# A two-layer hybrid decoder trunk on one core: boundaries reordered, modulation pieces behind the tile, level differences on VectorE, stick-breaking sums in two rounded parts

## The reference, cut to what matters

```python
def modulated_sublayer(x, fn, g_pre, g_post, m, res_w):
    shift, scale, gate = m[:, 0][:, None], m[:, 1][:, None], m[:, 2][:, None]
    h = rms_norm(x, g_pre) * (1.0 + scale) + shift
    return x + res_w * gate * rms_norm(fn(h), g_post)

for l in range(DEPTH):
    mod = (silu(c) @ w_ada[l] + b_ada[l]).reshape(bsz, 3, 3, D_MODEL)   # the modulation
    x = modulated_sublayer(x, ffn1,   ..., mod[:, 0], 0.5)   # (silu(h @ wa) * (h @ wb)) @ w_out
    x = modulated_sublayer(x, mixing, ..., mod[:, 1], 1.0)
    x = modulated_sublayer(x, ffn2,   ..., mod[:, 2], 0.5)
```

```python
log_1m = where(causal, log_sigmoid(-z), 0)            # minus the softplus of z
suffix = cumsum(log_1m, reverse=True) - log_1m
a = where(causal, exp(log_sigmoid(z) + suffix), 0);   o = a @ v
```

## Time and profile before

| | |
|---|---|
| median of three runs | 3118.58 us |
| the profiled execution's own time, and its span | 3121.1 us, 3119.3 us |
| mean granted TensorE clock | 0.975 of 2.4 GHz |
| PE busy | 2929.9 us (94%) |
| PE weight loads busy | 2558.1 us (82%) |
| DVE busy | 1541.3 us (49%) |
| ACT busy | 1005.0 us (32%) |
| POOL busy | 193.1 us (6%) |
| DMA | 324.53 MB, 104 GB/s on average |

### The profile page before, as it was taken

One profiled execution on the slowest core, in us unless ns is written; L12 is line 12 of the kernel. 1 busy time (PEld: TensorE's weight loads), 2 busy tenths in 40 slices (PEclk: granted clock), 3 DMA queues, 4 the chain that ended last, 5 costly groups with the idle time before them and its releaser, 6 DMA issues.

```text
span 3119.3 us, 40607 instructions
## 1 busy us (share of the span) xinstructions
PE 2929.9 (94%) x16999; PEld 2558.1 (82%) x16999; DVE 1541.3 (49%) x2236; ACT 1005.0 (32%) x1455; POOL 193.1 (6%) x188
## 2 busy tenths in 40 slices
PE   6999898989999988999989989899899999899998
PEld 5888897777788788889988879877777887888897
DVE  5555236777344446542255552477753554453323
ACT  3322124444422323222242221354443232332212
POOL 1000001221100020000000000021211002000000
PEclk7999999999999999999999999999999999999999
DMA  6555331222112233542226542222111232343321
GB/s 238 176 189 189 109 96 61 61 62 68 41 55 82 81 127 104 189 135 95 97 88 195 186 167 89 88 62 75 51 52 41 68 95 81 109 122 95 102 89 55
DMA packets 358854, 324.53 MB, mean 104 GB/s; under 512 B 12300, under 2 KB 305552, under 8 KB 357776
## 3 DMA queue, kind: packets, MB, share of 16 engines
q1 hardware_dynamic: 357136, 319.77, 32.4%
q10 hardware_dynamic: 1536, 2.16, 0.2%
HBM read 313.43 MB, written 6.29 MB: 102 GB/s over the span
## 4 chain that ended last, share of the span: by engine, by line
PE 85%; DVE 7%; ACT 3%; issue 2%; POOL 0%; ACTq 0%; DVEq 0%; POOLq 0%
PE PS L769 25%; PE PS L771 24%; PE PS L770 24%; PE PS L973 2%; PE PS L786 2%; DVE WL L1573 1%; PE PS L1048 1%; PE PS L1010 1%; PE PS L1070 1%; PE PS L1034 1%; PE PS L1025 1%; PE PS L1022 1%; PE PS L832 1%; ACT WH L1164 1%; PE PS L779 1%
## 5 line engine op out<-in xcount | busy, mean ns | idle before, releaser
L769 PE MATMUL PS<-HH,WH 128*128 128x512 f32 (+1 forms) x2512 | 974.3, 388 | 27.3 <-DVE WL L1562 10.3
L771 PE MATMUL PS<-HH,WL 128*128 128x512 f32 (+1 forms) x2512 | 948.7, 378 | 0.0
L770 PE MATMUL PS<-HL,WH 128*128 128x512 f32 (+1 forms) x2512 | 946.9, 377 | 0.0
L1562 DVE TENSOR_TENSOR WL<-RAW,WH 128x2048 fp32r<-128x2048 f32 x142 | 325.5, 2292 | 515.5 <-ACT WH L1164 515.5
L769 PEld LDWEIGHTS PS<-HH,WH 128*128 128x128 f32 x2512 | 475.7, 189 | 116.7 <-DVE WL L1573 13.7
L771 PEld LDWEIGHTS PS<-HH,WL 128*128 128x128 f32 x2512 | 475.0, 189 | 88.7
L770 PEld LDWEIGHTS PS<-HL,WH 128*128 128x128 f32 x2512 | 476.1, 190 | 82.0 <-issue 2.9
L1164 ACT ACTIVATE WH<-RAW 128x2048 fp32r<-128x2048 f32 x142 | 271.8, 1914 | 792.6 <-PE PS L771 792.6
L769 PE MATMUL PS<-GH,WH 128*128 128x256 f32 x1408 | 405.0, 288 | 18.2 <-DVE WL L1562 17.5
L771 PE MATMUL PS<-GH,WL 128*128 128x256 f32 x1408 | 403.7, 287 | 0.0
L770 PE MATMUL PS<-GL,WH 128*128 128x256 f32 x1408 | 403.3, 286 | 0.0
(11 more groups left out here) (225 smaller groups left out, 3470.3 us busy)
## 6 DMA issues: line engine op xcount, KB each, us to landing
RAW<-in_ffn_w_in SPq DMA_DIRECT2D x176, 512.0 KB, 5.2
RAW<-in_w_in SPq DMA_DIRECT2D x132, 512.0 KB, 4.7
AW<-in_w_ada SPq DMA_DIRECT2D x248, 256.0 KB, 4.8
RAW<-in_ffn_w_out SPq DMA_DIRECT2D x88, 512.0 KB, 4.2
AWB<-in_w_ada SPq DMA_DIRECT2D x5, 2048.0 KB, 16.0
RAW<-in_w_out SPq DMA_DIRECT2D x16, 512.0 KB, 4.0
x_kept<-X SPq DMA_DIRECT2D x2, 2048.0 KB, 7.4
X<-x_kept SPq DMA_DIRECT2D x2, 2048.0 KB, 10.1
```

What stands on the lines that cost most here:

```text
L769: pe.matmul(o, ah, bh, start=start, stop=skip, skip_group_check=skip)
L770: pe.matmul(o, ah, bl, start=False, stop=skip, skip_group_check=skip)
L771: return pe.matmul(o, al, bh, start=False, stop=stop or skip, skip_group_check=skip)
L1562: dve.tensor_tensor(wl[:, 0:n], RAW[g % 2][:, 0:n], wh[:, 0:n].bitcast(F32), ALU.subtract).then_inc(w_low, 1)
```

## The change

- **Buffers of the groups at a boundary.** `from_stage` gives a group's distance d to a stage's end. The group of d = -2 now goes into WXH[0], d = -1 and d = 0 into the other parity's WH, d = 1 into WXH[1]; the groups waited for are 2, 3, 3, 4, 3, 3 back for d = -2 to 3.
- **Order at a boundary.** ACT squares the updated x two steps earlier and takes the second root of y after the first two inputs are rounded; PE's sums of x for the second half stand at k = 3 to 5 instead of 4 to 7; a `rows_product` begins with banks 6 and 7, and waits by quarters. After the mixing the wait for all eight gate products (`br_mul`) is split as well.
- **Modulation.** In the first feed-forward part of a layer, the last chunk's sum on PE and its copy on DVE move behind the boundary, to step (3, 0) of the mixing.
- **Mixing.** `a_diff` is issued by DVE, one level ahead; `take` stands before `a_prepare`, whose step 3 is cut in two; transposes of turned values stand a step later; tiles 4 to 7 have banks of their own; the first weight group of `merge` gets its low part at step 3 of the last item.
- **Stick-breaking sums.** ACT rounds the masked softplus to BH (`b_round`), DVE takes the rest to BSL (`b_lows`), and `b_args` multiplies both with rounded copies of the matrices (CR).

The diff, cut to its core (lines that are only "..." are left out):

```diff
-    def beside(g):
-        return g % NG in (G_MIX, G_MIX + 1, G_FFN2, G_FFN2 + 1) or (g % NG < 2 and now[0] + g // NG > 0)
+    def from_stage(g):
+        g += NG * (now[0] > 0)
+        return min((g - e - n * NG for n in range(3) for e in ROW_ENDS if g - e - n * NG >= -2), default=99)
     def free(g):
-        if beside(g):
-            back = max((e for e in ROW_ENDS if e <= g), default=0) - 3
-        else:
-            back = g - (4 if beside(g - 2) else 2)
+        d = from_stage(g)
+        back = g - {-1: 3, 0: 3, 1: 4, 2: 3, 3: 3}.get(d, 2)
     def halves_of(g):
-        return (WXH[g % 2], WXL[g % 2]) if beside(g) else (WH[g % 2], WL[g % 2])
+        d = from_stage(g)
+        if d in (-2, 1):
+            return WXH[d > 0], WXL[d > 0]
+        slot = (g + (d in (-1, 0))) % 2
+        return WH[slot], WL[slot]
     def bank(tile):
-        return tile if tile < 4 else tile % 2
+        return tile if tile < 8 else tile % 2
...
                 def first_pair(p, g0, done):
-                            if not half and p and (u, i) == (1, 1) and k >= KT // 2:
-                                x_sum(p, 1, k - KT // 2)
+                            if not half and p and (u, i) == (1, 1) and 3 <= k <= 5:
+                                x_sum(p, 1, k - 3)
+                                if k == 5:
+                                    x_sum(p, 1, 3)
...
-                        for half in (1, 0) if i == 0 else (0, 1):
-                            for j in range(KT):
-                                if i == 0 and bank_free:
+                        for half, j0 in ((1, 4), (0, 0), (0, 4), (1, 0)) if i == 0 else ((0, 0), (0, 4), (1, 0), (1, 4)):
+                            for j in range(j0, j0 + 4):
+                                if i == 0 and j == j0:
                                     bank_free(half, j)
...
                 def b_args(h):
-                    pe.wait_ge(b_spm, at(b_spm, h + 1))
+                    pe.wait_ge(b_low, at(b_low, h + 1))
                     for i in range(TT):
-                        mm = pe.matmul(PS[:, bank, col:col + P], ident, const("negm"), ...)
-                        mm = pe.matmul(PS[:, bank, col:col + zw(i)], const("ntri"), BS[h % 2][:, ZCOL[i]:ZCOL[i] + zw(i)], ...)
-                        for j in range(i + 1, TT):
-                            mm = pe.matmul(PS[:, bank, col + P * (j - i):col + zw(i)], const("nones"),
-                                           BS[h % 2][:, ZCOL[j]:ZCOL[j] + zw(j)], ...)
+                        pe.matmul(PS[:, bank, col:col + P], CR[:, 0, :], CR[:, 3, :], ...)
+                        for j in range(i, TT):
+                            for part in (BH, BSL[h % 2]):
+                                mm = pe.matmul(PS[:, bank, col + P * (j - i):col + zw(i)], CR[:, 1 if j == i else 2, :],
+                                               part[:, ZCOL[j]:ZCOL[j] + zw(j)], ...)
...
+                def merged_free(half, j):
+                    pe.wait_ge(br_mul, at(br_mul, {(1, 4): KT - 2, (0, 0): KT - 1}.get((half, j), KT)))
                 def merged(i):
-                    if i == 0:
-                        pe.wait_ge(br_mul, at(br_mul, KT))
...
                     for m in range(2, NM):
                         for k in range(8):
+                            if (m, k) == (3, 0):
+                                pe.wait_ge(*taken(2))
+                                ada(0, ADA_CHUNKS[0] - 1)
...
# ScalarE
+                def b_round(h):
+                    act.wait_ge(b_spm, at(b_spm, h + 1))
+                    act.wait_ge(b_arg, at(b_arg, h))
+                    act.activation(BH[:, :], BS[h % 2][:, :], ACT.Copy).then_inc(b_high, 1)
...
# VectorE
+                def a_diff(h, k):
+                    n = A_LEVELS * h + k
+                    dve.wait_ge(p_log, at(p_log, 3 * h + 3))
+                    dve.wait_ge(v_decay, at(v_decay, max(n - 1, 0)))
+                    ...
+                    dve.tensor_tensor(level_view(AD[n % 2][:, :], k), b, b[:, :, w // 2 - 1:w // 2].broadcast_to(...), ALU.subtract)
                 def a_head(h, k):
+                    if k == 0:
+                        a_diff(h, 0)
+                    if k + 1 < A_LEVELS:
+                        a_diff(h, k + 1)
+                def b_lows(h):
+                    dve.wait_ge(b_high, at(b_high, h + 1))
+                    dve.tensor_tensor(BSL[h % 2][:, :], BS[h % 2][:, :], BH[:, :].bitcast(F32), ALU.subtract).then_inc(b_low, 1)
```

More of the change, by code:

```diff
@@ L158 @@
 _at = 0
-for _name, _n in (("ident", P), ("ones", P), ("ntri", P), ("nones", P), ("strict", P), ("negm", P),
+for _name, _n in (("ident", P), ("ones", P), ("ntri", P), ("nones", P), ("negm", P), ("strict", P),
                   ("reset", SEQ), ("del0", TT * 2 * P), ("del1", P), ("del2", P)):
@@ L319, in body @@
     BS = [sb(f"BS{i}", [P, 1280], F32, r1 + 34816 + 5120 * i) for i in range(2)]
+    BSL = [sb(f"BSL{i}", [P, 1280], F32R, r1 + 34816 + 5120 * i) for i in range(2)]
+    BH = sb("BH", [P, 1280], F32R, r1 + 12480)
+    CR = sb("CR", [P, 4, P], F32R, r1 + 57344)
     BA = [sb(f"BA{i}", [P, 1280], F32, r1 + 45056 + 5120 * i) for i in range(2)]
@@ L825, in ffn_in @@
                     first_pair(p, g0, lambda i: (a_done, w_used)[i])
-                    def ada(i):
-                        pe.wait_ge(ada_part, at(ada_part, i * KT + (ADA_BEFORE[f] + 2) * KT))
-                        pe.wait_ge(ada_out, at(ada_out, ADA_BEFORE[f] + i))
-                        for q in range(4):
-                            mm = pe.matmul(PS[:, 4, q:q + 1], AACC[i % 2][:, q * P:(q + 1) * P], ones[:, 0:1],
-                                           start=True, stop=True)
-                        mm.then_inc(ada_sum, 1)
                     n = chunks(l, f)
@@ L842, in ffn_in, with ada, rows_product @@
                             if u and i <= n:
[L843 to L847 removed]
+                                ada(f, i - 1)
+                def ada(f, i):
+                    pe.wait_ge(ada_part, at(ada_part, i * KT + (ADA_BEFORE[f] + 2) * KT))
+                    pe.wait_ge(ada_out, at(ada_out, max(ADA_BEFORE[f] + i - 1, 0)))
+                    for q in range(4):
+                        mm = pe.matmul(PS[:, ada_bank(f, i), q:q + 1], AACC[i % 2][:, q * P:(q + 1) * P], ones[:, 0:1],
+                                       start=True, stop=True)
+                    mm.then_inc(ada_sum, 1)
+                def rows_product(g0, n, rh, rl, ready, b, bank_free):
                     def column(i, j, half):
[L851 to L852 removed]
+                        wh, wl = (w[:, :].rearrange("p (k c) -> p k c", k=2) for w in halves_of(g0 + i))
                         cols = HALVES[half]
@@ L936, in project @@
                     tile = TILE0[m] + i
-                    if k0 == 0:
+                    if k0 == 0 and tile >= 8:
                         pe.wait_ge(tile_out[tile % 2], at(tile_out[tile % 2], tile // 2))
@@ L1241, in boundary @@
                         square_y(b, 1, q)
-                        if q in (1, 2) and not last:
-                            square_x(b + 1, 0, 2 * q - 2)
-                            square_x(b + 1, 0, 2 * q - 1)
-                    root_y(b, 1)
+                        if q < 2 and not last:
+                            square_x(b + 1, 0, 2 * q)
+                            square_x(b + 1, 0, 2 * q + 1)
                     if last:
+                        root_y(b, 1)
                         return
@@ L1587, in ffn_in @@
                                 ada_columns(f, i - 2)
+                            if (i, u) == (FI // 2 - 1, 1) and n == FI // 2:
+                                ada_columns(f, i - 1)
                             if i < n:
                                 ada_pieces(f, i, u)
-                    for i in range(min(n, FI // 2 - 2), n):
-                        ada_columns(f, i)
                 def ffn_tile(f, g0, i, u):
@@ L1878, in mixers @@
                         take(m, 0)
-                    if k == 2 and m and TILE0[m] - 1 in TURN_OF:
+                    if (m, k) in PREPARE_AT:
+                        a_prepare(*PREPARE_AT[(m, k)])
+                    if k == 3 and TILE0[m] - 1 in TURN_OF:
                         take_turned(TILE0[m] - 1)
```

85 lines of the change are left out of this document (46 added, 39 removed).

## The result

| | before | after |
|---|---|---|
| median of four runs | 3120.92 us | 2975.87 us |
| profiled execution, its span | 3121.1, 3119.3 us | 2976.25, 2974.5 us |
| PE busy | 2929.9 us | 2875.6 us |
| DVE, POOL busy | 1541.3, 193.1 us | 1555.2, 93.4 us |
| mean granted TensorE clock | 0.975 | 0.987 |

The ratio is 0.9534, 95% interval 0.9517 to 0.9550. The forecast was 2959, its range 2930 to 3010: the time lies in the range, inside the likeliest case's own 2940 to 2982, and on the number of the rival with dear matmuls (2976), whose mechanism isn't what happened. Between the two profiled spans lie 144.8 us where I had 160.

The account below looks back on a forecast made before the run. PE was taken to bound the kernel: its columns, its waits and its stretches at 1.2 GHz. The terms sum to 160 us off the profiled 3121.1, giving 2961, less 2.5 between profile and median 2959; range 2930 to 3010.

Parts of the forecast that it names:

- likeliest case: Whole kernel: forecast as summed, 2959 us, own range 2940 to 2982, chance 0.68.
- rival with dear matmuls: Stick-breaking sums: 128-column matmuls cost 0.23 us each, 17 us less gained, 2976 us; chance 0.12.
- a to e: Last two groups' buffers 40.2 us, boundary squares 12, boundary inputs 22, modulation's last chunk 21.9, merge and w_out 17.6.
- b: Squares of x at boundaries: PE's 2.4 us wait on XSQ goes at each of five; gain 12.0 us.
- c: Next sublayer's inputs: pair sums to second half's first matmul, 19.0 us instead of 23.4, five boundaries; gain 22 us.
- e: merge and w_out: waits on the low part and on the eighth gate product go; gains 11 and 6.6 us.
- one gap of about 2 us: Sign at the boundaries: one such PE gap in the first half of `first_pair`, none before the second.
- f: Stick-breaking sums: a head takes 3.1 us instead of 5.15, 12 heads; gain 24.4 us.
- hidden: Softplus, mask, rounding and low part before the sums need some 10.5 us, covered by PE's some 14 us of other work.
- g: A heads: 5 us from level copies, 17 from tiles and low parts, 3 from the clock; gain 25 us.
- The boundary's chain: Rival at the boundaries: ACT's and DVE's lists set the pace, (a) to (c) give 40, not 74; 2993 us; chance 0.15.
- DVE lost in the heads: Rival in A heads: the one level of lead is lost, 185 to 218 us lost, 3164 us; chance 0.03.

Follow-up runs that it names:

- undo_buffers: Changed kernel with the old choice of buffers for the last two groups of each of the six sublayers; 3013.58 us.
- undo_order: Changed kernel with the old order of squares, roots and x sums at the boundaries; 3012.87 us.
- undo_mod: Changed kernel with the modulation's last chunk summed at the end of ffn_in again, before the second stage; 2997.74 us.
- early_diff: Changed kernel with the first two level differences of a head computed by VectorE ahead of the take; 2962.37 us.
- early_highs: Changed kernel with ScalarE rounding the first two quarters of the next group before the first B head's softplus; 2970.59 us.
- undo_diff: Changed kernel with the seven level differences of a head issued by GpSimd again; 2991.58 us.
- undo_sums: Changed kernel with the stick-breaking sums back to fp32 products straight from the softplus, no rounding or low part; 2995.3 us.
- undo_takes: Changed kernel with VectorE's old list in the mixing, preparation ahead of the tile's copy, turned tiles a step earlier; own banks stay; 2982.59 us.
- only_diff: Kernel before the change with only the seven level differences of a head moved to VectorE; 3118.91 us, ratio 0.9994 to the kernel before.
- combined: Changed kernel with the early differences, early second low part, early rounded quarters and four more edits of VectorE's order; 2939.65 us.
- combined_token: `combined` with ScalarE also rounding the next group's first two quarters before head preparation in all items holding tokens' columns; 2931.95 us.

## Why the prediction was right, and where it was not

**a to e held, b and c in part by luck.** Waits counted times length from the earlier trace rows, half of PE's work in the half-clock stretches of the earlier trace rows, and for c the chain's new length, gave 113.7, and the stages show 114.3. `undo_buffers`, `undo_order` and `undo_mod` each brought back what the term said (38.6, 36.6 and 22.1 us of span), waits of the same kind included; e had no experiment of its own. The "one gap of about 2 us" came as 2.0, and the second half's start is covered. But from the pair sums' start to the second half's first matmul it takes 19.2 us at three boundaries and 20.5 at the two where the clock falls behind that gap, not 19.0 at all five, so c's chain gave 18.3 us and not 22. From the first half's pair sums to the second's it is 2.9 to 3.0 us shorter at each boundary where b had 2.4, 14.8 and not 12. The sum came out right because these two nearly cancel, with 1.6 us more where a later fall of the clock in one layer went.

**f: the sums were right, their cover was not.** A head's sums take 3.17 us (forecast 3.1). The Trainium skill, "TensorE: Matmul & The Clock Gate", section "Back-to-back issue gap", gives about 81 ns for 128 columns, by which my estimate was 2.8 us a head. This trace has 0.06 to 0.16 us from one matmul of 128 columns to the next in the sums at full clock, 0.10 in the mean. The step that failed is "hidden". I had 14 us of other work against a chain of 10.5. For the first head of a layer there is no neighbouring head's sum and value yet, so the work is 10.3 us, and the chain is 14.2 since weights' high and low parts and tiles stand between its links. `early_diff` shows the wait, 2.3 us in both layers (`early_highs` 2.2 in both, `undo_diff` 2.3 in one). With the clock up in both, the stage of the B heads takes 99.5 us in `early_diff` and 108.8 in `undo_sums`, 9.3 less for the new sums; without the wait it would be 11.6. The changed kernel doesn't show the wait because its clock is down there, and its stage takes 101.7, 2.2 more. That leaves 7.1 a layer against `undo_sums`, 6.7 against the kernel before (108.4), where I had 12.2.

**g: the total was 7 too high, because the new order brought a wait that I had at nothing.** I gave the differences 5 and the order of takes and banks 17. The level copies' wait fell by 6.3 (18.8 to 12.5), near the 5. Of the tiles' waits AV's 5.6 and VT's 5.2 went and BV's 6.6 fell to 3.7, 13.7 in all in place of 17; WL's 7.6, CV's 3.5 and GT's 2.8 stand as before. But PE now waits 5.4 more for QL (2.4 to 7.8), most of it in the first head of each layer. That wait belongs to the order and not to the differences: with the old order (`undo_takes`) it is 2.0, with the differences alone (`only_diff`) 2.0 too, and with the new order and the differences on GpSimd (`undo_diff`) 11.7. So the step that failed is "I take 17": 13.7 less 5.4, and `undo_takes` cost 6.3 (the tiles' own banks were not tried alone). "I take 5 of 18.8" holds between these two kernels, yet taken back beside the new order the differences cost 15.0, 10 of them the clock inside the heads. Together with the 6.3 that is more than the 15.0 that the change gained there, so the parts aren't additive. The rule I cited from the Trainium skill, "Perfetto Trace Analysis", section "Optimizing Scalar/DVE Operations", holds for its cause here (QL falls from 639 to 414 ns when the differences leave GpSimd). That such a move might not help is borne out by the medians of `only_diff` (1 us) and not by `undo_diff` (15.7). What still bound the heads was the order of DVE's list: it stood idle for 2.3 us before the take and was late 10 us later, which `early_diff` shows.

**The rivals.** Narrow matmuls dear: no, 0.10 us each in the mean and not 0.23; that the measured time is its 2976 is chance. The boundary's chain: no. DVE lost in the heads: no; the level copies' wait fell from 18.8 to 12.5, near the 14 I named.

## What to carry to other kernels

Count a wait's worth with the clock behind it, and leave room in the range for falls elsewhere: the same wait of 1.7 us was followed by 10 us at 1.2 GHz in nine layers and not in thirteen others, eleven kernels in all. When work is added to a pipelined chain, check the cover for its first round, where the neighbours that hide it don't exist yet. And on an engine with a strict list, look for idle time just before the place where it is late: moving two instructions a head into it was worth 10 us in the heads here. And an edit's worth found in one kernel isn't its worth in another: seven differences a head moved between the engines gave 15.0 us in the changed kernel and, by the medians, 1 in the kernel before.

## What the hardware showed that I had not expected

- The stretch of 10.2 us at half clock at the B heads' start came in nine of eighteen layers with the same wait of 1.7 us (the changed kernel and eight of its variants), in none of the four of the kernel before and `only_diff` with that wait, and without the wait in none of six (`early_highs`, `combined`, `combined_token`). Spans of one kernel's executions differ by up to 11.6 us, the longer at the lower mean clock (`undo_sums`).
- One fall hid a wait: at half clock PE was slow enough for the low part to be in time. The stage with the fall of 10.2 us is only 2.2 us longer than the one with the clock up and a wait of 2.3 (101.7 against 99.5 us).
- VectorE's products slow down while GpSimd computes the differences: QL, 128x256, takes 639 ns in the mean in `undo_diff` and 414 in the changed kernel, QB, 128x512, 1171 and 684. The difference itself, 128x512, takes 1.17 us on GpSimd there and 0.68 on VectorE.
